# Identity products at TensorE's long waits, wider columns of ones for sums over partitions, and two banks for the keys' tiles

## The chip, the cores and the metric

The kernel runs on one core of one Trainium2 chip. The metric is the device time of one execution in microseconds (us). The time before is 1876.21 us, the median of three runs (1876.06 to 1876.23).

## What is computed

The reference runs 256 tokens of width 1024 through two blocks in float32:

```python
def first_block(x, c, ...):                       # two layers
    for i in range(2):
        mod = silu(c) @ mod_w[i] + mod_b[i]       # shifts, scales and gates, 9 x 1024
        x = x + 0.5 * g1 * swiglu(modulate(rmsnorm(x), sh1, sc1), w13, w2)
        m = pool_ssd_mixer(h, ...) if i == 0 else mla_mixer(h, ...)
        x = x + g2 * m
        x = x + 0.5 * g3 * swiglu(modulate(rmsnorm(x), sh3, sc3), w13, w2)
    return rmsnorm(x, final_norm_g)

def second_block(x, mem, ...):
    x = x + hybrid_mixer(rms_norm(x, norm_mix_g), ...)   # convolution, compressed, selected and window attention
    x = x + cross_attention(rms_norm(x, norm_x_g), mem, ...)
    x = x + swiglu_2(rms_norm(x, norm_ffn_g), ...)
    return rms_norm(x, final_norm_g)
```

So the work is a chain of stages: a normalization, a product with streamed weights, something between the heads or channels, a product back, and the sum into x. Nothing of a stage can begin before x of the stage ahead is whole.

## The kernel before, in words

**Weights.** All weights come as one stream of blocks of 128 x 1024 numbers. SyncE loads them into a ring of six places (`raw`). ScalarE writes the rounded high part `w_hi` (L183, `split_hi`), VectorE the rest `w_lo` (L189, `split_lo`). A product of float32 accuracy is three matmuls in the float32r format (`triple`, L753): high by high, low by high, high by low. ScalarE may split block h only when block h - 6 has been multiplied (semaphore `used`), and SyncE may load over a place only when its low part has been taken. Every engine has one queue, in the order in which the program is written. In the second block, VectorE's queue also holds the 31 taps of a convolution along the tokens (`taps`, L2593 and L2597), three for each block of weights, written between the splits by `next_taps`.

**A normalization** (`norm_x` and `turn`) needs the squares of x (ScalarE), two steps on GpSimd for the root, and a diagonal matrix of the roots for each half of the tokens: the first from ScalarE (L509), the second from VectorE (L521). TensorE multiplies x by that diagonal, 8 tiles for each half (L621), which turns and scales it at once. VectorE and ScalarE take the tiles out of PSUM in pairs and split them (L643 to L682), and the next product starts at the first pair. In three of the normalizations TensorE also sums a block of modulations over the partitions between the two halves (`mod_turn`, L351): the moving operand there is one column of ones. TensorE's first instruction of a normalization waits for the first diagonal; what lies ahead of it in the queue is the last product of the stage before.

**The state-space mixer** of layer 0 handles eight parts n (four quads of heads, two halves of the tokens). For each n, TensorE spreads the running sums (`sums_on_all_rows`, L1571), runs half a block of another product (`z_half`), waits for VectorE's decays (L1614) and multiplies them (`outputs`, L1637 and L1640). After the last one come the sums of squares over the partitions (`group_sums`, L1731) and the roots on all rows (`group_scale`, L1755), in the middle of the product back (`rows_product`).

**The second block's mixer.** `columns_product` multiplies eight convolution pairs, two pairs for the compressed keys and values, then the two sets of keys (`evac_keys`, L2633: four copies on ScalarE for one pair) and the queries. It takes banks ps4 and ps5 in turn by `pair % 2`, counted anew in each call, so two calls of one pair each both take ps4. Then come the products of the compression (`L2664`, 60 columns, and `L2668`, one column), two products for the values, the scores against the compressed keys (L2802, 15 columns), their softmax on VectorE and ScalarE (L2823 to L2854), its transposes (L2866), and 32 passes of attention (`pass_scores`, `pass_turn` L2961, `pass_values` L2980 and L2983), each with half a block of another product (`fill_half`). Within the passes the squares of the convolution are summed by one column of ones (`deviation_sums`, L3044). After the last pass the convolution's channels are split (`conv_split`, L3117) for the next product.

## Time and profile before

| | before |
|---|---|
| median of three runs | 1876.21 us |
| the profiled execution's own time | 1879.29 us |
| its span, first to last instruction | 1877.4 us |
| TensorE busy | 1747.7 us (93%) |
| VectorE busy | 1253.4 us (67%) |
| ScalarE busy | 880.9 us (47%) |
| mean granted TensorE clock | 0.968 |

Busy times are sums over an engine's instructions, and a matmul's end is modelled, so TensorE's 93% is not a share of its peak. [...] A float32 product of a 128 x 128 tile (the L621, L351, L1731 and L3044 kinds) stands in the trace as two records.

### The profile page before, as it was taken

The numbers are of one execution on the slowest core, as the hardware profiler recorded it, in microseconds if no ns is written. First come the engines' busy times: TensorE is split into PE (matmuls) and PEld (weight loads), VectorE is DVE, ScalarE is ACT, GpSimd is POOL, SyncE is SP. The second block draws the span as 40 slices with busy tenths as digits, with TensorE's granted clock in tenths as the row PEclk, the third lists the DMA queues.
The fourth block names the chain that finished last, engine by engine and source line by source line (L and its number), as shares of the span: only waits on it lengthen the run. The fifth ranks groups of instructions, "written<-read, shape, count | busy, mean of one in ns | idle before, by whom it ended". The sixth has DMA issues, their size and how long they took to land.

```text
span 1877.4 us, 32609 instructions
## 1 busy us (share of the span) xinstructions
PE 1747.7 (93%) x11926; PEld 1601.4 (85%) x11926; DVE 1253.4 (67%) x2120; ACT 880.9 (47%) x1412; POOL 72.0 (4%) x119
## 2 busy tenths in 40 slices
PE   4899999799999999999989999898999899899998
PEld 4799988778999889998778999788977688779997
DVE  5777878558778778766556555599785465455554
ACT  1444457534444434444664444545255554554443
POOL 1000001100000000000000000100000000000000
PEclk9999999989999999999999999899799999999999
DMA  9798857647988688854335655344332155326652
GB/s 349 252 304 294 288 140 199 138 163 250 305 296 288 175 324 300 292 170 135 113 91 156 190 183 182 129 146 148 106 92 72 46 180 180 112 79 207 185 184 73
DMA packets 123655, 352.75 MB, mean 188 GB/s; under 512 B 9850, under 2 KB 52874, under 8 KB 114224
## 3 DMA queue, kind: packets, MB, share of 16 engines
q1 hardware_dynamic: 108128, 262.18, 44.3%
q10 hardware_dynamic: 12432, 78.65, 12.3%
q0 software_dynamic: 3008, 10.74, 1.7%
q8 instruction: 58, 0.95, 0.2%
q14 instruction: 29, 0.24, 0.0%
HBM read 347.31 MB, written 4.22 MB: 187 GB/s over the span
## 4 chain that ended last, share of the span: by engine, by line
PE 75%; DVE 13%; ACT 6%; issue 4%; DMA 2%; POOL 1%; ACTq 0%; DVEq 0%; POOLq 0%
PE ps L753 64%; DVE w_lo L189 3%; ACT w_hi L183 2%; DVE arena L2597 2%; PE ps L621 2%; PE ps L2983 1%; PE ps L351 1%; PE ps L2903 1%; DVE arena L342 1%; DMA arena<-in_small 1%; DVE resid L1166 1%; DMA arena<-in_mod_w 1%; PE ps L2961 1%; DVE tmp L1163 0%; DVE act_s L1163 0%
## 5 line engine op out<-in xcount | busy, mean ns | idle before, releaser
L753 PE MATMUL ps<-t_hi,w_hi 128*128 128x256 f32 (+1 forms) x2616 | 757.7, 290 | 21.1 <-DVE arena L2597 5.3
L753 PE MATMUL ps<-t_hi,w_lo 128*128 128x256 f32 (+1 forms) x2616 | 748.9, 286 | 0.0
L753 PE MATMUL ps<-t_lo,w_hi 128*128 128x256 f32 (+1 forms) x2616 | 748.9, 286 | 0.0
L753 PEld LDWEIGHTS ps<-t_hi,w_hi 128*128 128x128 f32 (+1 forms) x2616 | 507.8, 194 | 39.5 <-issue 18.0
L753 PEld LDWEIGHTS ps<-t_lo,w_hi 128*128 128x128 f32 (+1 forms) x2616 | 508.5, 194 | 2.1
L753 PEld LDWEIGHTS ps<-t_hi,w_lo 128*128 128x128 f32 (+1 forms) x2616 | 508.3, 194 | 0.3
L1027 DVE TENSOR_TENSOR w_lo<-raw,w_hi 128x1024 fp32r<-128x1024 f32 x258 | 313.8, 1224 | 155.8 <-ACT w_hi L1016 155.8
L189 DVE TENSOR_TENSOR w_lo<-raw,w_hi 128x1024 fp32r<-128x1024 f32 x240 | 289.7, 1225 | 176.6 <-ACT w_hi L183 176.5
L1016 ACT ACTIVATE w_hi<-raw 128x1024 fp32r<-128x1024 f32 x258 | 269.2, 1053 | 175.1 <-PE ps L753 174.7
L183 ACT ACTIVATE w_hi<-raw 128x1024 fp32r<-128x1024 f32 x240 | 249.0, 1053 | 154.2 <-PE ps L753 129.4
L753 PE MATMUL ps<-w_hi,g_hi 128*128 128x512 f32 x440 | 175.7, 399 | 6.2 <-DVE g_lo L1058 6.1
L342 DVE SCALAR_TENSOR_TENSOR arena<-arena,cact 128x512 f32<-128x512 f32 x231 | 173.2, 750 | 5.1
L753 PE MATMUL ps<-w_hi,g_lo 128*128 128x512 f32 x440 | 172.2, 391 | 0.0
L753 PE MATMUL ps<-w_lo,g_hi 128*128 128x512 f32 x440 | 171.7, 390 | 0.0
L1034 ACT ACTIVATE act_s<-ps 128x256 f32<-128x256 f32 x110 | 42.1, 383 | 194.4 <-PE ps L753 194.4
L753 PE MATMUL ps<-w_hi,t_hi 128*128 128x512 f32 (+1 forms) x272 | 106.1, 390 | 3.4 <-ACT arena L2185 1.5
L753 PEld LDWEIGHTS ps<-w_hi,g_hi 128*128 128x128 f32 x440 | 82.8, 188 | 25.0 <-issue 9.1
L753 PE MATMUL ps<-w_lo,t_hi 128*128 128x512 f32 (+1 forms) x272 | 103.1, 379 | 0.0
L753 PE MATMUL ps<-w_hi,t_lo 128*128 128x512 f32 (+1 forms) x272 | 103.0, 379 | 0.0
L2597 DVE SCALAR_TENSOR_TENSOR arena<-arena,cols 128x256 f32<-128x256 f32 x240 | 99.2, 491 | 0.0
L753 PEld LDWEIGHTS ps<-w_lo,g_hi 128*128 128x128 f32 x440 | 82.7, 188 | 17.9
L1036 ACT ACTIVATE g_hi<-act_s 128x256 fp32r<-128x256 f32 x110 | 45.9, 417 | 110.7 <-DVE act_s L1055 110.7
(337 smaller groups left out, 1656.6 us busy)
## 6 DMA issues: line engine op xcount, KB each, us to landing
raw<-in_stream SPq DMA_DIRECT2D x498, 512.0 KB, 4.4
arena<-in_mod_w ACTq DMA_DIRECT2D x72, 1024.0 KB, 7.2
grow<-gate_scratch POOLq DMA_DIRECT2D x6, 512.0 KB, 9.0
u_scratch<-u_keep ACTq DMA_DIRECT2D x1, 3072.0 KB, 33.8
arena<-u_scratch POOLq DMA_DIRECT2D x8, 256.0 KB, 3.3
small<-in_small POOLq DMA_DIRECT2D x1, 1368.0 KB, 24.9
resid<-in_x POOLq DMA_DIRECT2D x1, 1024.0 KB, 17.0
arena<-in_mem POOLq DMA_DIRECT2D x1, 1024.0 KB, 5.6
```

The source lines that it names most:

```text
L183: E.activation(w_hi[:, s, :], raw[:, s, :], ACT.Copy).then_inc(hi_done, 1)
L189: VE.tensor_tensor(w_lo[:, s, :], raw[:, s, :], w_hi[:, s, :].bitcast(F32), ALU.subtract).then_inc(lo_done, 1)
L342: VE.scalar_tensor_tensor(out=total, in0=w, scalar=cact[:, k:k + 1], in1=total, op0=ALU.mult, op1=ALU.add).then_inc(mod_step, 1)
L351: last = TE.matmul(ps[7][:, at + j:at + j + 1], total[:, j * P:(j + 1) * P], cs("ones", 0, 1), start=True, stop=True)
L621: last = TE.matmul(in_bank(kt)[:, q * P:(q + 1) * P], src(q)[:, kt * P:(kt + 1) * P], rstd_diag[:, q, :], start=True, stop=True)
L753: last = TE.matmul(out, lhs, rhs, start=start and i == 0, stop=stop and i == 2)
L1016: E.activation(w_hi[:, s, :], raw[:, s, :], ACT.Copy).then_inc(hi_done, 1)
L1027: VE.tensor_tensor(w_lo[:, s, :], raw[:, s, :], w_hi[:, s, :].bitcast(F32), ALU.subtract).then_inc(lo_done, 1)
L1034: E.activation(act_s[:, t, 0:L], ps[4 + t][:, 0:L], ACT.Silu).then_inc(silu_done, 1)
L1036: E.activation(g_hi[:, t, :], act_s[:, t, L:2 * L], ACT.Copy).then_inc(gate_hi, 1)
L1166: VE.tensor_tensor(x[:, q, fs], x[:, q, fs], product[:, f, :], ALU.add).then_inc(V.sem, V.up())
L2597: VE.scalar_tensor_tensor(out=cv[:, tile, :], in0=cin[:, tile, k:k + L], scalar=col("dw_w", 8 * k + tile), in1=cv[:, tile, :], op0=ALU.mul ...
```

## The change

It puts four things into TensorE's queue or takes them out:

- `keep_busy(bank, n)` multiplies the identity by itself n times into a bank that nobody reads. It stands ahead of the wait in seven of the normalizations (8, 4, 8, 8, 20, 40 and 36 times), in the state-space parts 1 to 6 (5 each) and 7 (12), at the group sums (6), at the scores (12, and three times 2 between them), at the turns of passes 0 and 31 (6 each) and ahead of the convolution's last product (26). These are 228 products.
- The sums over the partitions use 64 columns of ones (modulations) or 128 (the rest) in place of one. The readers take every 64th or 128th column.
- The compression's one-column products read 60 columns, and 24 of 32 score products 30 columns in place of 15; the added columns are not read.
- The second set of keys takes ps5 (`shift=1`).

```diff
-            total, at = (modp_first[c], 4 * c) if first else (modp, place)
+            total = modp_first[c] if first else modp
             for j in range(4):
-                last = TE.matmul(ps[7][:, at + j:at + j + 1], total[:, j * P:(j + 1) * P], cs("ones", 0, 1), start=True, stop=True)
+                at, wide = (4 * c + j, 1) if first else (place + 64 * j, 64)
+                last = TE.matmul(ps[7][:, at:at + wide], total[:, j * P:(j + 1) * P], cs("ones", 0, wide), start=True, stop=True)
...
                     if kt == 0 and qs[0] == 0:
+                        keep_busy(ps[4], busy)
                         pe.wait_ge(A.sem, entry[1])
...
+        def keep_busy(bank, n):
+
+            for _i in range(n):
+                TE.matmul(bank[:, 0:P], ident, ident, start=True, stop=True)
...
-                bank = ps[4 + pair % 2]
+                which = (pair + shift) % 2
+                bank = ps[4 + which]
...
                 else:
                     pe.wait_ge(A.sem, small_at["state"])
+                if n == 7:
+                    pe.wait_ge(V.sem, less_at[6])
+                if n:
+                    keep_busy(ps[3 if n < 7 else 6], 5 if n < 7 else 12)
                 pe.wait_ge(V.sem, decay_at[n])
...
+                keep_busy(ps[6], 6)
                 pe.wait_ge(A.sem, max(square_at[3], rows_at[7]))
...
-                            last = TE.matmul(ps[7][:, 2 * g + q:2 * g + q + 1], zT[:, 4 * g + i, q * P:(q + 1) * P],
-                                             cs("ones", 0, 1), start=i == 0, stop=i == 3)
+                            last = TE.matmul(ps[7][:, (2 * g + q) * P:(2 * g + q + 1) * P], zT[:, 4 * g + i, q * P:(q + 1) * P],
+                                             cs("ones"), start=i == 0, stop=i == 3)
...
-        columns_product(2, evac_keys(1), chained=True)
+        columns_product(2, evac_keys(1), chained=True, shift=1)
...
-                    last = TE.matmul(cmp_pos[kind][0:64, 0:1], w, sm("pos", kind * 16 + lp, kind * 16 + lp + 1),
+                    last = TE.matmul(cmp_pos[kind][0:64, 0:60], w, sm("pos", kind * 16 + lp - 59, kind * 16 + lp + 1),
...
+            keep_busy(ps[6], 12)
             pe.wait_ge(A.sem, kcmp_at[0])
...
+                    n_col = N_CMP if h // 4 == 3 else 2 * N_CMP
+                    last = TE.matmul(ps[4 + h % 2][:, c:c + n_col], qT[b:b + 64, h // 2, q * P:(q + 1) * P],
+                                     kcmp[b:b + 64, (h // 4) * N_CMP:(h // 4) * N_CMP + n_col], start=True, stop=True)
+                    if h % 8 == 7 and (q, h) != (QT - 1, HEADS - 1):
+                        keep_busy(ps[6], 2)
...
+                pe.wait_ge(A.sem, pt_kept.get(n - 2, pc_at))
+                if n in (0, N_PASS - 1):
+                    keep_busy(ps[4 + n % 2], 6)
                 pe.wait_ge(V.sem, scaled[n])
-                pe.wait_ge(A.sem, pt_kept.get(n - 2, pc_at))
...
-                        last = TE.matmul(sum_bank(1)[:, q:q + 1], square[:, k, q * P:(q + 1) * P], cs("ones", 0, 1),
+                        last = TE.matmul(sum_bank(1)[:, q * P:(q + 1) * P], square[:, k, q * P:(q + 1) * P], cs("ones"),
...
+                    if (pr, half) == (0, 0):
+                        keep_busy(bank, 26)
                     pe.wait_ge(lo_done, h + 1)
```

`token_sums` (L2027) is widened in the same way as L3044. The places of the seven calls in the normalizations, in the order of the program, are those whose L621 starts at 259, 427, 636, 847, 996, 1197 and 1601 us of the trace before.

The order of TensorE's queue at the normalization ahead of the second block's mixer (L621 at 1197 us). Names are output bank <- operands; a row without a wait stands right behind the one ahead. Before:

```order
L753 MATMUL ps<-w_hi,g_hi 128x512
L753 MATMUL ps<-w_hi,g_lo 128x512
L753 MATMUL ps<-w_lo,g_hi 128x512
L598 UNCONDITIONAL_BRANCH
L621 MATMUL ps<-arena,resid 128x128 [waits vector_steps,scalar_steps]
```

With the change (keep_busy is L755, `triple` L761, the product by the diagonal L624):

```order
L761 MATMUL ps<-w_hi,g_hi 128x512
L761 MATMUL ps<-w_hi,g_lo 128x512
L761 MATMUL ps<-w_lo,g_hi 128x512
L600 UNCONDITIONAL_BRANCH
L755 MATMUL ps<-cst 128x128 x40
L624 MATMUL ps<-arena,resid 128x128 [waits vector_steps,scalar_steps]
```

Forty products without a wait of their own now stand between the feed-forward's last matmul and the wait for the diagonal.

The order of TensorE's queue from the compression's last products to the scores (before):

```order
L2705 MATMUL ps<-arena,small 64x60 [waits scalar_steps]
L2708 MATMUL ps<-small,arena 15x64 [waits scalar_steps]
L2708 MATMUL ps<-small,arena 15x64 x3
L2795 UNCONDITIONAL_BRANCH
L2802 MATMUL ps<-arena 128x15 [waits scalar_steps]
L2802 MATMUL ps<-arena 128x15 x31
```

With the change:

```order
L2723 MATMUL ps<-arena,small 64x60 [waits scalar_steps]
L2726 MATMUL ps<-small,arena 15x64 [waits scalar_steps]
L2726 MATMUL ps<-small,arena 15x64 x3
L2813 UNCONDITIONAL_BRANCH
L755 MATMUL ps<-cst 128x128 x12
L2822 MATMUL ps<-arena 128x30 [waits scalar_steps]
L2822 MATMUL ps<-arena 128x30 x7
L755 MATMUL ps<-cst 128x128 x2
L2822 MATMUL ps<-arena 128x30 x4
L2822 MATMUL ps<-arena 128x15 x4
L755 MATMUL ps<-cst 128x128 x2
```

Twelve identity products stand ahead of the wait for the compressed keys, and two more after every eight score products but the last.

## Rows read from the trace of the kernel before

**Rows 1.** The page: its span and the busy time of each engine.

```profile
span 1877.4 us, 32609 instructions
...
PE 1747.7 (93%) x11926; PEld 1601.4 (85%) x11926; DVE 1253.4 (67%) x2120; ACT 880.9 (47%) x1412; POOL 72.0 (4%) x119
```

**Rows 2.** Windows over the stretches at 0.50: columns from, to, length, busy per engine, PEclk, DMA; then their sum.

```profile
376.81:387.06 10.25, 8.93 (x38) 7.49 (x39) 3.10 (x5) 2.01 (x3) 0.00 (x0) 0.50 0.12 42
...
390.47:397.30 6.83, 6.83 (x21) 5.67 (x22) 0.16 (x1) 0.00 (x0) 1.05 (x1) 0.50 0.24 77
...
663.54:666.95 3.41, 3.41 (x19) 3.41 (x18) 2.43 (x3) 1.16 (x2) 0.00 (x0) 0.50 1.02 425
...
1192.60:1202.84 10.24, 5.64 (x26) 5.67 (x27) 4.01 (x8) 4.70 (x13) 3.71 (x6) 0.50 0.01 2
...
1318.89:1335.96 17.07, 17.07 (x133) 17.05 (x132) 11.50 (x26) 2.61 (x6) 2.25 (x3) 0.50 0.39 118
...
1448.60:1455.43 6.83, 6.83 (x26) 5.09 (x26) 3.60 (x14) 1.86 (x6) 1.67 (x1) 0.50 0.26 77
...
1489.56:1492.97 3.41, 3.20 (x11) 2.10 (x11) 0.15 (x1) 0.49 (x1) 0.00 (x0) 0.50 0.00 0
...
sum 121.60, PE 108.60 PEld 102.37 DVE 54.25 ACT 35.62 POOL 15.49; mean PE 5.17 PEld 4.87 DVE 2.58 ACT 1.70 POOL 0.74
```

**Rows 3.** Timeline, TensorE: start, length, line, shape, records; in brackets idle before and releaser.

```profile
427.14 2.02 PE L621 MATMUL ps<-arena,resid 128*128 128x128 f32 x16 [1.50 <-DVE resid L1166]
...
635.79 3.35 PE L621 MATMUL ps<-arena,resid 128*128 128x128 f32 x16 [2.09 <-DVE resid L1166]
...
996.01 6.41 PE L621 MATMUL ps<-arena,resid 128*128 128x128 f32 x32 [3.48 <-DVE resid L1166]
...
1197.20 6.50 PE L621 MATMUL ps<-arena,resid 128*128 128x128 f32 x32 [6.62 <-ACT arena L509]
```

**Rows 4.** Timeline, VectorE, in the normalization whose transposes start at 1197.20.

```profile
1198.74 0.29 DVE L521 TENSOR_SCALAR arena<-cst,st 128x128 f32<-128x128 f32 x1 [2.54 <-POOL st L498]
...
1201.42 0.48 DVE L643 TENSOR_SCALAR tmp<-ps,cols 128x256 f32<-128x256 f32 x1 [2.39 <-PE ps L621]
```

**Rows 5.** Timeline, TensorE, heads of the state-space stage.

```profile
348.01 0.45 PE L1637 MATMUL ps<-arena 128*64 128x128 f32 x4 [2.01 <-DVE arena L1614]
...
355.21 0.66 PE L1637 MATMUL ps<-arena 128*64 128x128 f32 x8 [0.59 <-DVE arena L1614]
...
361.83 0.45 PE L1637 MATMUL ps<-arena 128*64 128x128 f32 x4 [2.02 <-DVE arena L1614]
...
377.35 0.70 PE L1637 MATMUL ps<-arena 128*64 128x128 f32 x4 [2.75 <-DVE arena L1614]
```

**Rows 6.** Timeline, TensorE, sums by one column of ones, and the next work.

```profile
1444.92 3.73 PE L3044 MATMUL ps<-cst,arena 128*128 128x1 f32 x32
...
1448.51 0.82 PE L2961 MATMUL ps<-cst,act_s 128*128 128x128 f32 x3
```

**Rows 7.** Timeline, TensorE, from the keys to the scores.

```profile
1280.55 0.36 PE L753 MATMUL ps<-t_hi,w_hi 128*128 128x256 f32 x1 [2.63 <-DVE arena L2597]
...
1319.54 3.51 PE L2668 MATMUL ps<-small 128*64 128x1 f32 x32
...
1347.03 4.69 PE L2802 MATMUL ps<-arena 64*128 64x15 f32 x64 [1.96 <-ACT arena L2717]
```

**Rows 8.** Windows, then VectorE's timeline, in the same stage.

```profile
1240.00:1330.00 90.00, 79.62 (x641) 78.23 (x640) 90.00 (x185) 37.29 (x49) 0.95 (x1) 0.90 0.46 145
...
1339.98 1.23 DVE L189 TENSOR_TENSOR w_lo<-raw,w_hi 128x1024 fp32r<-128x1024 f32 x1 [9.60 <-ACT w_hi L183]
...
1353.88 0.61 DVE L2823 TENSOR_TENSOR act_s<-ps,biasc 128x120 f32<-128x120 f32 x2
```

**Rows 9.** Timeline, TensorE, after the softmax and after the last pass.

```profile
1360.71 1.09 PE L2866 MATMUL ps<-cst,act_s 128*128 128x128 f32 x8 [0.94 <-DVE act_s L2854]
...
1497.62 0.55 PE L753 MATMUL ps<-t_hi,w_hi 128*128 128x256 f32 x1 [4.36 <-DVE t_lo L3117]
```

More of the change, by code:

```diff
@@ L358, in mod_add @@
                 else bass.ds(c * 4 + COL["mod_b"][0], 4)
-            VE.tensor_tensor(modc[:, sl], ps[7][:, place:place + 4], cols[:, bl], ALU.add).then_inc(mod_added, 1)
+            sums = ps[7][:, place:place + 256].rearrange("p (a b) -> p a b", b=64)[:, :, 0]
+            VE.tensor_tensor(modc[:, sl], sums, cols[:, bl], ALU.add).then_inc(mod_added, 1)
         @block.scalar
@@ L530, in turn @@
         def turn(src, n_kt, segs=None, scale=None, shift=None, kt0=0, dst=None, ready=None, done=False, mods_before=0, early=4,
-                 columns=None, late_mod=None, late_load=False):
+                 columns=None, late_mod=None, late_load=False, busy=0):
             src_ready = ready or {(q, f): V.n for q in range(QT) for f in range(2)}
@@ L911, in columns_product @@
                 evac(pair, bank)
-                bank_free[pair % 2] = (V.n if V.n > at_v else 0, A.n if A.n > at_a else 0)
+                bank_free[which] = (V.n if V.n > at_v else 0, A.n if A.n > at_a else 0)
                 next_split()
@@ L1169, in _, with norm_x @@
                         x_ready[q, f] = V.n
-        def norm_x(gain, mods=None, ready=None, mods_before=0, early=4, late_mod=None, late_load=False):
+        def norm_x(gain, mods=None, ready=None, mods_before=0, early=4, late_mod=None, late_load=False, busy=0):
             if mods is not None:
@@ L1189, in norm_x @@
                      dst=lambda q: ar(XN, QT, D)[:, q, :], ready=ready or dict(x_ready), done=ready is not None,
-                     mods_before=mods_before, early=early, columns=gain_and_scale, late_mod=late_mod, late_load=late_load)
+                     mods_before=mods_before, early=early, columns=gain_and_scale, late_mod=late_mod, late_load=late_load, busy=busy)
             else:
                 turn(lambda q: x[:, q, :], KT, [(0, D)], lambda k: gain(k, 1), None,
-                     dst=lambda q: ar(XN, QT, D)[:, q, :], ready=dict(x_ready), early=early)
+                     dst=lambda q: ar(XN, QT, D)[:, q, :], ready=dict(x_ready), early=early, busy=busy)
         def mod_at(layer, which):
@@ L1203, in build @@
         ffn(0, FG, PRE, (mod_at(0, 2), 0.5))
-        norm_x(lambda k, n: col("norm_g", 8 + k, n), (mod_at(0, 3), mod_at(0, 4)), early=2, late_mod=PRE + FG - 1)
+        norm_x(lambda k, n: col("norm_g", 8 + k, n), (mod_at(0, 3), mod_at(0, 4)), early=2, late_mod=PRE + FG - 1, busy=8)
         xb = ar(0, 12, 259)
@@ L1738, in _ @@
                 dve.wait_ge(T.sem, at)
-                VE.tensor_scalar(wide, ps[7][:, 0:4], 1.0 / 512, EPS, ALU.mult, ALU.add).then_inc(V.sem, V.up())
+                VE.tensor_scalar(wide, ps[7][:, :].rearrange("p (a b) -> p a b", b=P)[:, :, 0], 1.0 / 512, EPS, ALU.mult,
+                                 ALU.add).then_inc(V.sem, V.up())
             at = V.n
@@ L1915, in _ @@
                         out_done[h] = V.n
-        norm_x(lambda k, n: col("norm_g", 32 + k, n), (mod_at(1, 3), mod_at(1, 4)), early=2)
+        norm_x(lambda k, n: col("norm_g", 32 + k, n), (mod_at(1, 3), mod_at(1, 4)), early=2, busy=8)
         squared = ar(0, 4, 512)
@@ L2016, in square_pair, with sums_of @@
             squared_at[i] = A.n
+        def sums_of(bank, at):
+            return bank[:, at * P:(at + 2) * P].rearrange("p (a b) -> p a b", b=P)[:, :, 0]
         def token_sums(pairs, bank, at, read=0):
@@ L2026, in _ @@
                     for i, tile in enumerate(tiles):
-                        last = TE.matmul(bank[:, at + q:at + q + 1], tile, cs("ones", 0, 1), start=i == 0,
+                        last = TE.matmul(bank[:, (at + q) * P:(at + q + 1) * P], tile, cs("ones"), start=i == 0,
                                          stop=i == len(tiles) - 1)
@@ L2466, in build @@
         add_residual((mod_at(1, 5), 1.0))
-        norm_x(lambda k, n: col("norm_g", 40 + k, n), (mod_at(1, 6), mod_at(1, 7)))
+        norm_x(lambda k, n: col("norm_g", 40 + k, n), (mod_at(1, 6), mod_at(1, 7)), busy=20)
         first_gain = ar(0, D)
@@ L2511, in build @@
         norm_rows(first_gain)
-        norm_x(lambda k, n: col("mix", k, n), early=2)
+        norm_x(lambda k, n: col("mix", k, n), early=2, busy=40)
         qT = ar(0, KT, L)
@@ L2675, in _ @@
                 act.wait_ge(T.sem, cmp_mm[kind])
-                E.activation(zk[0:64, 60:61], cmp_pos[kind][0:64, 0:1], ACT.Copy).then_inc(A.sem, A.up())
+                E.activation(zk[0:64, 60:61], cmp_pos[kind][0:64, 59:60], ACT.Copy).then_inc(A.sem, A.up())
                 act.wait_ge(A.sem, A.n)
@@ L2801, in _ @@
                     c = q * 256 + (h // 2) * 32
-                    last = TE.matmul(ps[4 + h % 2][:, c:c + N_CMP], qT[b:b + 64, h // 2, q * P:(q + 1) * P],
-                                     kcmp[b:b + 64, (h // 4) * N_CMP:(h // 4 + 1) * N_CMP], start=True, stop=True)
+                    n_col = N_CMP if h // 4 == 3 else 2 * N_CMP
[3 more added lines that the diff above has]
+                        keep_busy(ps[6], 2)
             last.then_inc(T.sem, T.up())
@@ L3256, in build @@
         evac_rows(vx, ACT.Copy)
-        norm_x(lambda k, n: col("nx", k, n))
+        norm_x(lambda k, n: col("nx", k, n), busy=36)
         columns_product(8, evac_q(qx))
```

18 lines of the change are left out of this document (9 added, 9 removed).

## The prediction

> **What bounds the kernel now.** I read the page first: TensorE is busy 93% of the span, VectorE 67%, ScalarE 47% [rows 1]. So TensorE's queue sets the time, except where it waits. [...] The stretches lie behind waits and behind one-column sums. The timeline then says, stretch by stretch, who is late: the diagonal of a normalization [rows 3], VectorE's decays [rows 5], the taps in VectorE's queue [rows 7, 8]. Two prices follow. At half clock 26 records of L621 fill 5.64 us [rows 2], 0.217 each. The 32 one-column records of L3044 run 1444.92 to 1448.51 at full clock, 0.112 each [rows 6]; 128-column L621 records at full clock I take at the same. So wider ones cost TensorE nothing, and an identity product (two records) costs 0.224 us at full clock, 0.434 at half: 228 of them are 51 us. They are free only inside a wait. That decides each place.
>
> **The change, part by part** (gain positive).
>
> *Normalizations.* At 1197.20 the first copy out of PSUM, which starts the next product, begins at 1201.42, 4.22 after the first L621 [rows 4]. It needs 18 records, and 4.22 less 18 x 0.217 leaves 0.31. At full clock the same is 18 x 0.112 + 0.31 = 2.33. The second diagonal is ready 1.83 after the start (1199.03) [rows 4], so it does not gate. Full clock is worth 1.9. Against it stands the overrun, fills less wait. Eight fills (1.8) fit the wait of 2.09 at 636, where the clock fell just behind the start [rows 2, 3]; two more places, 259 and 847, have the same kind of wait. I take 1.5 each, 4.5 together. Four fills (0.9) fit the 1.50 at 427, where nothing was slow: 0. Twenty (4.5) overrun the 3.48 at 996 by 1.0: +0.9. Forty (9.0) overrun 6.62 by 2.3: -0.4. I take the same -0.4 for the 36 at 1601. Sum **4.6**. Should a fill be shorter than 0.224, the two long ones gain.
>
> *State-space.* Of the two late stretches TensorE fills 8.93 + 6.83 = 15.8 us [rows 2], worth 7.9. Twelve fills (2.7) fit the wait of 2.75 [rows 5]; six at the group sums (1.3) I charge in full. Two of the 21 windows, 3.41 us each, lie in earlier parts, and a part with one took 7.20 (348.01 to 355.21) against 6.62 without (355.21 to 361.83) [rows 5]: 0.6 each. Five fills (1.1) fit the waits near 2.0 and overrun the one of 0.59 by 0.5, which I charge once, as the next wait takes up the rest. 7.9 - 1.3 + 1.2 - 0.6 = **7.2**.
>
> *Columns of ones.* The fall at 663.54 comes right behind the modulations' one-column sums, with 3.41 us of work in it [rows 2]: **1.5**. A like one lies behind the latent's sums (L2027): **1.4**. At 1448.60 the clock falls right behind L3044, with no idle ahead [rows 6]; 6.83 us of busy work follow: **3.1**. VectorE now reads with a stride, 2 to 4 elements: 0.
>
> *Keys to scores.* On TensorE alone much could go: the second set of keys waits 2.63 for its bank [rows 7] and once more alike; two short falls follow, each like the one at 663.54 [rows 2] and worth 1.7; the long stretch from 1318.89 is 17.07 us [rows 2], but of it only the weights' product at the end gains (2.9), since the compression's records are spaced 3.51/32 = 0.110 at half clock [rows 7], the spacing of full clock elsewhere. Together 2 x 2.63 + 2 x 1.7 + 2.9 = 11.6. But VectorE is busy 90.00 of 90 us here [rows 8], with taps and splits in one queue, and what TensorE gains it can only turn into an earlier end of that queue. Its next idle is the 9.60 ahead of 1339.98, released by ScalarE's split, and that by TensorE [rows 8]. When that idle is gone, VectorE's chain from 1339.98 to the softmax at 1353.88, 13.9 us, stays. The ends are 0 (the queue is the bound already) and 9.6 (the idle vanishes). 11.6 exceeds it, so I take **9.6**. The 18 fills there (4.0, wait 1.96) cost nothing while the scores, done at 1351.7 before [rows 7], still end ahead of VectorE's arrival.
>
> *After the softmax.* TensorE, early now, waits longer at L2866 (0.94 before [rows 9]), by what it gains over VectorE: some 4 us, with no fill. I expect the clock to fall there in place of a little later, where it fell before: **0**.
>
> *Passes and end.* The fall at 1489.56 holds 3.20 us of work, the wait of 4.36 ahead of 1497.62 comes behind it [rows 2, 9]. TensorE's and the chain's share of a steady clock is 1.8, the convolution's product itself 0.6 (it is paced by `conv_split`, so 26 fills, 5.8, overrun 4.36 at no price): **2.5**. At pass 0 `pt_kept` and the wait's order change nothing that is late.
>
> Sum 4.6 + 7.2 + 1.5 + 1.4 + 3.1 + 9.6 + 2.5 = 29.9. Every later stage shifts in time, and places without a fill (the latent's short waits, pass 1 onward) may now see a fall: I charge one, 2.0. Gain **27.9**. The profiled execution took 1879.29, span 1877.4; 1851.4 by its count. The median of the runs is 3.1 lower, so **1848.3**. A measurement of this kernel tells some 0.2% (3.8 us) from no change.
>
> [...] The trace's side: from 1192.60 to 1202.84 nothing ran but 26 records of L621, and then the clock rose [rows 2, 3].
>
> **The rivals.**
>
> 1. *VectorE's queue is the bound to the softmax.* For: busy 90.00 of 90 [rows 8]. Against: the idle of 9.60 is there. The keys' term is 0: 1848.3 + 9.6 = 1858. Chance 0.14.
>
> 2. *New falls.* The clock's falls move rather than go, as it does in waits the table of fills leaves out. Four more of 2.2 each (half of 3.4 to 6.8 us [rows 2], less what is hidden): 1857. For: many stretches began behind waits of a microsecond or less. Chance 0.13.
>
> 3. *One-column sums are not what lets the clock fall.* Then the ones give nothing: 1.5 + 1.4 + 3.1 less, 1854.3. [...] Against this rival: [rows 6] has 32 records without a gap and then the fall. Chance 0.08.
>
> 4. *Identity products don't hold the clock (slower).* The mechanism is at the seven normalizations and the other filled waits: the clock falls while they run, so each takes 0.434 and they overrun. Normalizations: 3 x (3.5 - 2.1) + 0.2 for the four at 427 + (8.7 - 3.5) + (17.4 - 6.6) + (15.6 - 5.9) = 30.1; state-space, 12 and 6 fills: 2.4 + 2.6; the last product 11.3 - 4.4 = 6.9. That is 42.0 lost, less 5.3 for the keys' second bank: 1876.2 + 36.7 = 1913. It decides from some 0.39 us per fill on: 162 fills stand where the wait is already full, and 27.9/162 = 0.17 more for each takes the gain. Against it speaks the rise at 1202.84. Chance 0.05.
>
> **How the numbers follow.** The forecast has 0.60. Its own unknowns are the overruns (0 to 4), the shared VectorE chain and the passes' end (0 to 5): 1841 to 1853. Rivals 1 to 3 lie at 1854 to 1858, two of them together at 1863. Nothing prices better than 1838: it needs the whole 11.6 and no overrun and no new fall. So 1838 to 1863 leaves out rival 4 and combinations, some 0.15. Faster by over 0.2% are all but rival 4 and a tail: 0.92; within 0.2% 0.03; slower 0.05.
>
> **What the later profile would show.** Right, if TensorE's mean granted clock rises from 0.968 to 0.99; if the identity products stand 0.112 us per record at clock 1.00; if the diagonal's products in the normalizations start right behind the last fill, with no idle in the long two, and the first copy comes 2.3 after; if L3044 keeps its length with 128 columns and no fall follows; if TensorE has no wait left at the second keys; and if VectorE's idle of 9.60 is gone while the softmax stands 13.9 behind that split. The step after the softmax is right if TensorE waits about 4 us there. The forecast is wrong if the 9.60 stays (rival 1), if stretches at 0.50 sum to more than 40 us (2), if a fall still stands behind the wide sums (3), or if identity products run at 0.217 per record (4).

## The result, and the profile after

| | before | after |
|---|---|---|
| median | 1876.22 us (4 runs, 1876.06 to 1876.71) | 1851.97 us (4 runs, 1850.26 to 1854.25) |
| ratio after to before | | 0.9866, 95% interval 0.9852 to 0.988 |
| the profiled execution's own time | 1879.29 us | 1850.26 us |
| mean granted clock | 0.968 | 0.996 |

The change makes the kernel 24.25 us faster by the medians and 29.0 us faster by the two profiled executions. A second measurement of the changed kernel, beside other kernels on another occasion, gave a median of 1853.85 us.

The page of the changed kernel, its span and busy times, answers to [rows 1]:

```profile
span 1848.4 us, 33513 instructions
PE 1758.8 (95%) x12382; PEld 1615.3 (87%) x12382; DVE 1252.6 (68%) x2120; ACT 880.2 (48%) x1412; POOL 72.6 (4%) x119
```

TensorE has 456 more records (228 identity products) and is busy 11 us longer in a span that is 29 us shorter. In every trace of this case the granted clock is either 1.00 ("full clock" here) or 0.50 ("half clock"). The windows over the stretches at 0.50, which answer to [rows 2]; the columns are those of [rows 2]:

```profile
1200.70:1204.13 3.43, 3.43 (x19) 3.43 (x18) 1.23 (x1) 0.60 (x1) 0.00 (x0) 0.50 0.78 287
1323.60:1333.84 10.24, 10.24 (x62) 9.92 (x63) 10.14 (x23) 0.00 (x0) 0.00 (x0) 0.50 0.47 139
```

Of 121.6 us at half clock, 13.67 are left, and a last stretch from 1845.85 on, behind TensorE's final product (1841.24). The longer one lies at the scores. The window ahead of it:

```profile
1316.78:1323.60 6.82, 6.82 (x76) 6.29 (x76) 6.82 (x15) 5.25 (x10) 0.00 (x0) 1.00 0.36 102
```

TensorE was busy for 6.82 of 6.82 us, mostly with the twelve fills and the first scores of 30 columns, and the clock went from 1.00 to 0.50 at 1323.60 all the same. Without any fills (the first experiment below) a stretch of 10.24 us stands there too, from 1325.17 on. So the fills at the scores show no effect.

TensorE's timeline at the fills and the diagonal's products behind them, in the normalizations that stood at 259, 996, 1197 and 1601 (two of them in [rows 3]):

```profile
258.00 1.95 PE L755 MATMUL ps<-cst 128*128 128x128 f32 x16
260.25 2.02 PE L624 MATMUL ps<-arena,resid 128*128 128x128 f32 x16 [0.30 <-DVE resid L1175]
...
979.16 4.62 PE L755 MATMUL ps<-cst 128*128 128x128 f32 x40
983.63 3.74 PE L624 MATMUL ps<-arena,resid 128*128 128x128 f32 x32
...
1175.80 9.09 PE L755 MATMUL ps<-cst 128*128 128x128 f32 x80
1184.73 3.74 PE L624 MATMUL ps<-arena,resid 128*128 128x128 f32 x32
...
1566.06 8.20 PE L755 MATMUL ps<-cst 128*128 128x128 f32 x72
1574.09 3.74 PE L624 MATMUL ps<-arena,resid 128*128 128x128 f32 x32
```

Eight fills leave 0.30 us of the wait; the long ones leave none. Eighty records take 1184.73 - 1175.80 = 8.93 us, 0.112 each, as priced. The 32 records of the products by the diagonal, 6.50 us before, now take 3.74. ScalarE's first diagonal and VectorE's first copy at 1184.73:

```profile
1182.05 0.40 ACT L511 ACTIVATE arena<-cst,st 128x128 f32<-128x128 f32 x1 [0.37 <-POOL st L500]
```

```profile
1186.94 0.93 DVE L646 TENSOR_SCALAR tmp<-ps,cols 128x256 f32<-128x256 f32 x2 [2.52 <-PE ps L624]
```

The diagonal was ready at 1182.45, the fills ended 2.3 us later, and the first copy comes 2.21 after the first product; the forecast had 2.33. The convolution's sums with 128 columns, TensorE's timeline, answer to [rows 6]:

```profile
1420.88 3.84 PE L3068 MATMUL ps<-cst,arena 128*128 128x128 f32 x32
```

They take 3.84 us in place of 3.73, and no fall follows: the clock is 1.00 from 1333.84 to 1845.85. Last the stage from the keys to the softmax, which answers to [rows 8]: a window, then VectorE's last splits and the softmax.

```profile
1240.00:1330.00 90.00, 86.73 (x763) 85.00 (x763) 90.00 (x185) 41.11 (x59) 3.20 (x4) 0.96 0.48 150
```

```profile
1317.12 1.23 DVE L189 TENSOR_TENSOR w_lo<-raw,w_hi 128x1024 fp32r<-128x1024 f32 x1
...
1331.02 1.18 DVE L2845 TENSOR_TENSOR act_s<-ps,biasc 128x120 f32<-128x120 f32 x4
```

The split that waited 9.60 us has no idle ahead of it, and the softmax starts 13.9 us behind it, as before. VectorE is busy without a break.

**Where the time came from.** VectorE runs the same instructions in the same order in both kernels, so the start of the same instruction, after less before, shows stage by stage what was gained. From the two traces, beside the forecast:

| place | forecast | measured |
|---|---|---|
| normalizations at 259, 636, 847 | 4.5 | 1.5 + 1.4 + 0.8 = 3.7 |
| at 996, 1197, 1601 | 0.9 - 0.4 - 0.4 | 1.3 + 0.1 + 0.7 |
| state-space | 7.2 | 7.2 |
| modulations' and latent's sums | 1.5 + 1.4 | 1.2 + 1.6 |
| a new fall behind L883 (1200.7) | in the 2.0 charged | -1.2 |
| keys to softmax | 9.6 | 9.7 |
| after the softmax | 0 | 0.9 |
| passes, convolution's sums | 3.1 | 3.3 |
| end of the passes | 2.5 | 1.4 |
| sum | 27.9 | 29.0 (0.7 was lost in the first 62 us, 0.1 behind the last place) |

### The profile page after: what moved, and what is told of

It is laid out like the page before. It is cut to its first block, busy times and chain, and to the rows that moved or that the text cites. A ratio compares the mean times of both kernels' runs of the same rounds, so it can differ in the third digit from the quotient of the medians.

```text
span 1848.4 us, 33513 instructions
## 1 busy us (share of the span) xinstructions
PE 1758.8 (95%) x12382; PEld 1615.3 (87%) x12382; DVE 1252.6 (68%) x2120; ACT 880.2 (48%) x1412; POOL 72.6 (4%) x119
## 4 chain that ended last, share of the span: by engine, by line
PE 73%; DVE 14%; ACT 6%; issue 5%; DMA 2%; POOL 0%; ACTq 0%; DVEq 0%; POOLq 0%
PE ps L761 63%; DVE w_lo L189 4%; DVE arena L2615 3%; ACT w_hi L183 2%; PE ps L352 1%; PE ps L755 1%; PE ps L3007 1%; PE ps L2925 1%; DVE arena L342 1%; DMA arena<-in_small 1%; PE ps L624 1%; DMA arena<-in_mod_w 1%; DVE resid L1175 1%; PE ps L2985 1%; ACT t_hi L674 0%
## 5 line engine op out<-in xcount | busy, mean ns | idle before, releaser
L761 PE MATMUL ps<-t_hi,w_hi 128*128 128x256 f32 (+1 forms) x2616 | 751.0, 287 | 14.5 <-DVE t_lo L685 6.1
L761 PE MATMUL ps<-t_lo,w_hi 128*128 128x256 f32 (+1 forms) x2616 | 743.0, 284 | 0.0
L761 PE MATMUL ps<-t_hi,w_lo 128*128 128x256 f32 (+1 forms) x2616 | 742.8, 284 | 0.0
L761 PEld LDWEIGHTS ps<-t_hi,w_hi 128*128 128x128 f32 (+1 forms) x2616 | 502.3, 192 | 31.3 <-issue 14.4
L761 PEld LDWEIGHTS ps<-t_lo,w_hi 128*128 128x128 f32 (+1 forms) x2616 | 502.5, 192 | 2.1
L761 PEld LDWEIGHTS ps<-t_hi,w_lo 128*128 128x128 f32 (+1 forms) x2616 | 502.4, 192 | 0.2
L761 PE MATMUL ps<-w_hi,g_hi 128*128 128x512 f32 x440 | 175.7, 399 | 6.0 <-DVE g_lo L1067 5.7
L761 PE MATMUL ps<-w_hi,g_lo 128*128 128x512 f32 x440 | 172.1, 391 | 0.0
L761 PE MATMUL ps<-w_lo,g_hi 128*128 128x512 f32 x440 | 171.7, 390 | 0.0
L761 PE MATMUL ps<-w_hi,t_hi 128*128 128x512 f32 (+1 forms) x272 | 102.8, 378 | 3.4 <-ACT arena L2203 1.6
L761 PEld LDWEIGHTS ps<-w_hi,g_hi 128*128 128x128 f32 x440 | 82.8, 188 | 25.1 <-issue 9.1
L761 PE MATMUL ps<-w_lo,t_hi 128*128 128x512 f32 (+1 forms) x272 | 100.1, 368 | 0.0
L761 PE MATMUL ps<-w_hi,t_lo 128*128 128x512 f32 (+1 forms) x272 | 100.0, 368 | 0.0
L761 PEld LDWEIGHTS ps<-w_lo,g_hi 128*128 128x128 f32 x440 | 82.6, 188 | 18.1
```

The lines of the kernel that those rows point to most:

```text
L761: last = TE.matmul(out, lhs, rhs, start=start and i == 0, stop=stop and i == 2)
```

## The experiments

Twelve kernels ran, in three groups of four, each group beside runs of the kernel before. That kernel's median was 1878.88, 1875.98 and 1878.97 in the three, with single runs from 1872.99 to 1884.13, so kernels of different groups are compared by their ratio to it. The changed kernel's ratio was 0.9866 first and 0.988 in the second group.

### Take the fills away

```diff
         def keep_busy(bank, n):
-            for _i in range(n):
-                TE.matmul(bank[:, 0:P], ident, ident, start=True, stop=True)
+            return
```

> The changed kernel without its 228 identity products; wide columns and the keys' second bank stay. My theory (the fills hold the clock through their waits): the terms of the normalizations (4.6), most of the state-space stage (4 to 7) and the end of the passes (2.5) are lost: 1863 to 1866, and the profile shows falls to 0.50 again at 259, 636, 847, 996, 1197, 1497 and 1601 of the kernel before. Rival (the fills bring nothing, the wide columns and the bank do it all): 1850 to 1854, with the overruns of the long fills gone.

Measured: 1860.82 us, ratio 0.9911 (0.9883 to 0.9939). The changed kernel's ratios were 0.9866 and 0.988, so the fills are worth 0.3 to 0.45% of the time, 6 to 8 us, less than the 11 to 14 expected. TensorE's timeline in the normalization that stood at 1197, and VectorE's first copy:

```profile
1188.25 5.63 PE L624 MATMUL ps<-arena,resid 128*128 128x128 f32 x32 [6.63 <-ACT arena L511]
```

```profile
1192.35 0.93 DVE L646 TENSOR_SCALAR tmp<-ps,cols 128x256 f32<-128x256 f32 x2 [2.27 <-PE ps L624]
```

The clock falls there again (0.50 from 1185.22 to 1192.05), and the first copy comes 4.10 after the first product in place of 2.21. But the product starts 0.15 behind the diagonal in place of 2.28, since nothing overruns. The forty fills give nothing and cost nothing, close to the term -0.4. Laid over the changed kernel, 8.2 us are lost without the fills: 1.6 at the normalization at 259, 1.6 in the state-space stage, 2.4 between 640 and 685, where the modulations of the next stage are summed, 1.3 at the end of the passes, and the rest in pieces below 1. Of the 2.4, 1.3 stands at a fall (673.23, 3.4 us at 0.50) that the changed kernel's second trace has too (671.03), with its fills. From that first copy to the softmax the time is 144.01 us against 144.08: in that stage the fills do nothing.

At three places where the forecast put the gain down to the fills, it is there without them. TensorE's timeline of this kernel at the normalization that stood at 636 and at the late part of the state-space stage, beside 635.79 in [rows 3] and 377.35 in [rows 5]:

```profile
630.50 2.02 PE L624 MATMUL ps<-arena,resid 128*128 128x128 f32 x16 [2.12 <-DVE resid L1174]
...
377.45 0.45 PE L1649 MATMUL ps<-arena 128*64 128x128 f32 x4 [2.74 <-DVE arena L1622]
```

The waits are as long as before, nothing fills them, and the clock stays at 1.00 (3.35 and 0.70 us before). Against the kernel before, this one gains 1.5 us at 636, 0.8 at 847 and 5.6 in the state-space stage, where the changed kernel gained 1.4, 0.8 and 7.2. My expectation of falls at 636 and 847 missed. Part of the 5.6 is the group sums' 128 columns (1.6, shown below); the rest is not tied to any edit.

### Fills that stream one column

```diff
-                TE.matmul(bank[:, 0:P], ident, ident, start=True, stop=True)
+                TE.matmul(bank[:, 0:1], ident, ident[:, 0:1], start=True, stop=True)
```

> The changed kernel with identity products that stream one column in place of 128; as many records, in the same places. They should stand 0.11 us apart as before. My theory (what counts for the clock is what is streamed, not that the queue is occupied): the clock falls at the filled places as without fills, and the overruns of the long fills stay on top: 1865 to 1870. Rival (occupied time holds the clock): 1850 to 1854.

Measured: 1876.95 us, ratio 0.9986 (0.9972 to 1.0001): hardly faster than before. TensorE's timeline and two windows at the forty fills:

```profile
1186.43 15.06 PE L755 MATMUL ps<-cst 128*128 128x1 f32 x80
1201.36 4.87 PE L624 MATMUL ps<-arena,resid 128*128 128x128 f32 x23
```

```profile
1184.00:1188.62 4.62, 4.62 (x33) 4.19 (x31) 4.51 (x8) 2.17 (x6) 1.21 (x2) 1.00 0.00 0
1188.62:1205.69 17.07, 17.07 (x81) 17.07 (x82) 3.15 (x7) 3.79 (x11) 3.70 (x6) 0.50 0.00 1
```

TensorE is busy without a gap, the clock falls among the fills, at 1188.62, and is 0.50 for 17.07 us. The last 4.3 of them, from 1201.36 on, hold 128-column products. Of the 14.93 us from the first fill to the diagonal's product, 21 records at full clock take 2.4; the other 59 stand 0.213 apart. So the forty end 6 us later than the wide ones. TensorE's queue was occupied here for all of the 17.07 us at 0.50; with the same number of records of 128 columns, at the same place, the clock was 1.00 over the whole 8.93 us. The direction was expected, not the size (1865 to 1870): the forecast for this run took 0.11 us per record at either clock.

### Fills issued as transposes

```diff
-                TE.matmul(bank[:, 0:P], ident, ident, start=True, stop=True)
+                TE.transpose(bank[:, 0:P], ident, ident)
```

> The changed kernel with its fills issued as transposes of the identity in place of plain matmuls by it, the same number and places. [...] If they count as a matmul does: 1850 to 1855 and a clock of 0.99.

Measured: 1849.99 us, ratio 0.9841 (0.9824 to 0.9857). TensorE's timeline, then two windows:

```profile
1180.62 4.53 PE L755 MATMUL ps<-cst 128*128 128x128 f32 x40
1187.41 5.44 PE L624 MATMUL ps<-arena,resid 128*128 128x128 f32 x32 [2.25 <-ACT arena L511]
```

```profile
1184.90:1188.31 3.41, 1.16 (x11) 0.94 (x10) 1.42 (x2) 1.84 (x7) 2.00 (x4) 1.00 0.00 0
1188.31:1191.73 3.42, 3.42 (x19) 3.42 (x18) 0.84 (x3) 0.47 (x1) 0.56 (x1) 0.50 0.02 5
```

A transpose is one record of 0.112 us where the float32 product is two, so forty take half the time and leave an idle of 2.25. The clock is 1.00 for as long as they run and falls only behind that idle. Idle at this place let the clock fall 2.0 us after its start in the kernel before (1190.58 to 1192.60) and 3.6 us after it without fills (1181.62 to 1185.22); here the clock stood for the 7.7 us from 1180.62 to 1188.31, with nothing in them but the transposes, the idle and 0.9 us of L624. So over these 4.53 us the transposes held the clock at 1.00, as the identity products did over their 8.93 in the changed kernel, and the runs (median 1849.99, clocks 0.989 to 0.994) are close to the 1850 to 1855 and 0.99 expected for transposes that count as a matmul does. The kernel is no slower than with the long fills, though the clock falls behind the short ones (0.50 from 1188.31 to 1191.73), which fits the forty being too many.

### One column of ones again

```diff
-                at, wide = (4 * c + j, 1) if first else (place + 64 * j, 64)
+                at, wide = (4 * c + j, 1) if first else (place + 64 * j, 1)
...
-                        last = TE.matmul(sum_bank(1)[:, q * P:(q + 1) * P], square[:, k, q * P:(q + 1) * P], cs("ones"),
+                        last = TE.matmul(sum_bank(1)[:, q * P:q * P + 1], square[:, k, q * P:(q + 1) * P], cs("ones", 0, 1),
```

> The changed kernel with one column of ones again in the four kinds of sums over partitions; the fills, the 60 and 30 columns and the keys' second bank stay. My theory (work that streams one column lets the clock fall, though TensorE has no idle): 1.5 + 1.4 + 3.1 are lost, 1857 to 1859, with falls behind the modulations' sums near 650, the latent's near 856 and the convolution's sums near 1423. Rival (only idle lowers the clock, the wide columns are idle talk): 1850 to 1854 and no fall at those three places.

Measured: 1861.0 us, ratio 0.9902 (0.9877 to 0.9927), 4 to 7 us above the changed kernel (0.988 and 0.9866). TensorE's timeline at the convolution's sums, and the windows around:

```profile
1429.79 3.86 PE L3068 MATMUL ps<-cst,arena 128*128 128x1 f32 x32
1433.51 0.88 PE L2985 MATMUL ps<-cst,act_s 128*128 128x128 f32 x3
```

```profile
1426.00:1433.25 7.25, 7.25 (x56) 6.18 (x55) 2.16 (x12) 3.90 (x11) 0.00 (x0) 1.00 0.29 86
1433.25:1440.08 6.83, 6.83 (x26) 5.09 (x26) 3.55 (x14) 1.87 (x6) 1.67 (x1) 0.50 0.26 77
```

TensorE is busy 7.25 of 7.25 us and the clock falls at 1433.25; with the same 32 records of 128 columns (3.84 us, from 1420.88 on in the changed kernel) it stayed at 1.00. That stage alone lost 3.0 us, the term 3.1. All three traces with one column here have this fall (at 1448.60, 1433.25 and 1444.79, 6.83 us each), and none of the eleven with 128 columns has one. The falls at the group sums (388.77, 1.6 us lost) and the latent's sums (859.81, 1.2 lost), 3.41 us at 0.50 each, came back too.

The one near 650 did not, and for the modulations' sums the runs do not show that the column count is the cause. All traces have a wait of 1.1 us ahead of that sum. With one column the clock fell in one trace of three, with 64 in none of eleven. At the next sum, 17 us on, it fell in eight of the eleven with 64 columns, at waits of 1.45 to 2.77 us, and stood in the three others, at 0.76, 1.13 and 2.19.

The profiled execution is 12.1 us above the changed kernel's. Its other losses stand where this edit changes nothing: 1.3 near 81 us (0.50 from 78.16 to 81.57) and 4.5 from the scores to the first passes, where the clock is 0.50 for 13.65 us.

### The keys in one bank, and narrow compression, singly and together

```diff
-        columns_product(2, evac_keys(1), chained=True, shift=1)
+        columns_product(2, evac_keys(1), chained=True)
```

> The changed kernel with both sets of keys in the same bank again. My theory: VectorE's queue sets the time from the keys to the softmax; without the second bank TensorE loses 2 x 2.63 there, of which VectorE's idle takes a part: 1854 to 1858, and an idle of 2 to 5 us stands again ahead of a low split in VectorE's queue between 1300 and 1320. Rival (the fills and wider columns alone fill VectorE's queue): 1850 to 1854. Rival (the bank is the whole 9.6): 1861.

```diff
-                    last = TE.matmul(cmp_pos[kind][0:64, 0:60], w, sm("pos", kind * 16 + lp - 59, kind * 16 + lp + 1),
+                    last = TE.matmul(cmp_pos[kind][0:64, 59:60], w, sm("pos", kind * 16 + lp, kind * 16 + lp + 1),
...
-                    n_col = N_CMP if h // 4 == 3 else 2 * N_CMP
+                    n_col = N_CMP
```

> The changed kernel with one column again in the compression's second products and 15 in all the scores. No second bank explains more than a part of the 9.6, as the kernel without it showed 2.5. My theory now: most of the rest came from the clock held through the compression; here it falls there again, TensorE's next products are late by 3 to 6 and VectorE's idle ahead of the last splits is back: 3 to 6 above the changed kernel. Rival (VectorE's queue hides it all): 0 to 1 above, with a fall but no idle on VectorE.

Both diffs at once:

> The changed kernel with the keys in one bank and the compression and scores narrow again, both at once. From the first copy of the normalization at 1197 to the softmax it was 152.5 us before, 144.1 with the change, 146.6 without the bank and 145.8 with the narrow columns. Theory (both make slack on TensorE ahead of a VectorE queue that is the bound, and each makes most of it): together more than the sum 2.5 + 1.7, that stretch at 149 to 153 and VectorE's idle back at 6 to 10. Rival (they add): 148.3.

| kernel | median us | ratio (95% interval) | first copy to softmax |
|---|---|---|---|
| before | | 1 | 152.46 |
| changed (second measurement) | 1853.85 | 0.988 (0.9866 to 0.9894) | 144.08 |
| one bank | 1856.03 | 0.9879 (0.9854 to 0.9905) | 146.59 |
| narrow | 1851.77 | 0.9876 (0.9858 to 0.9893) | 145.75 |
| both | 1857.75 | 0.9888 (0.987 to 0.9905) | 148.72 |

The times of whole kernels do not tell these apart, the stage does. VectorE's timeline with one bank, the split ahead of which the idle stands and the softmax:

```profile
1321.38 1.23 DVE L189 TENSOR_TENSOR w_lo<-raw,w_hi 128x1024 fp32r<-128x1024 f32 x1 [2.31 <-ACT w_hi L183]
...
1335.40 0.91 DVE L2845 TENSOR_TENSOR act_s<-ps,biasc 128x120 f32<-128x120 f32 x3
```

The bank is worth 2.5 us, nearly all of it as an idle of VectorE that is back. The narrow columns cost 1.7 there (3 to 6 were expected), though all 17.07 us at half clock are back (1300.07 to 1317.14); VectorE's queue hides most of them. Together they cost 4.6, about the sum, where I had expected more than the sum. So 3.7 of the 8.4 us of this stage come back neither with both edits nor without the fills alone (144.01); all three edits at once weren't tried. The traces say where most of it lies. TensorE's timeline at the compression's second products, before [rows 7], with the change, and with both edits undone:

```profile
1319.54 3.51 PE L2668 MATMUL ps<-small 128*64 128x1 f32 x32
...
1297.63 2.04 PE L2686 MATMUL ps<-small 128*64 128x60 f32 x32
...
1304.55 1.99 PE L2686 MATMUL ps<-small 128*64 128x1 f32 x32
```

Before, both sets of 32 ran at half clock, 3.51 us each. With both edits undone they took 1.99 and 2.15 us, one column or not: 1.5 and 1.4 less. The clock fell mostly between them, from 1306.73 to 1310.14, 0.4 us into the second set, and again at the scores, from 1330.62 on. So where the falls happen to lie decides, and not these two edits alone.

### The changed kernel again, with shorter fills, with fewer taps

```diff
-        norm_x(lambda k, n: col("norm_g", 40 + k, n), (mod_at(1, 6), mod_at(1, 7)), busy=20)
+        norm_x(lambda k, n: col("norm_g", 40 + k, n), (mod_at(1, 6), mod_at(1, 7)), busy=16)
...
-        norm_x(lambda k, n: col("mix", k, n), early=2, busy=40)
+        norm_x(lambda k, n: col("mix", k, n), early=2, busy=30)
...
-        norm_x(lambda k, n: col("nx", k, n), busy=36)
+        norm_x(lambda k, n: col("nx", k, n), busy=27)
```

> The changed kernel, unchanged, as the measure for the other three of this group. Every theory: 1850 to 1855, some 23 to 25 below the kernel before. Its runs should scatter by about 4 us, since the places where the clock falls depend on what happens to lie together.

> The changed kernel with 30, 27 and 16 identity products in place of 40, 36 and 20 in the three longest normalization waits. In the trace of the changed kernel the last fill ends 2.2, 2.0 and 0.9 us after the first diagonal there. My theory (the long fills overrun, and what the clock gives they take): the first copy out of PSUM comes 2.1, 1.9 and 0.9 earlier, 4.9 in all: 4 to 5 below the changed kernel, if the clock does not fall in the rest of the wait. Rival (another engine is as late, or the shorter row lets the clock fall): no gain.

Measured: the changed kernel 1853.85 us (1853.42 to 1854.56), with shorter fills 1850.02 (1848.06 to 1850.7), ratios 0.988 and 0.9856 (0.9842 to 0.9871): 3.8 us less. TensorE's timeline with thirty fills:

```profile
1179.66 6.86 PE L755 MATMUL ps<-cst 128*128 128x128 f32 x60
1186.42 3.94 PE L624 MATMUL ps<-arena,resid 128*128 128x128 f32 x32
```

The clock is 1.00 from the first fill to the end of the products, and the product starts as the fills end. The overrun was real: beside the repeated changed kernel the first copy comes 2.0 us earlier here, and 1.8 us earlier at 1601. The rest of the difference is not the fills' alone. This trace has a fall in the state-space stage that the other lacks (0.50 from 351.76 to 355.17, 2.1 us lost), and it lacks the one behind L883 (0.50 from 1203.51 to 1206.93 in the other, 1.5 gained), though the wait there is the same 1.80 us:

```profile
1201.64 0.32 PE L883 MATMUL ps<-cst,tmp 48*128 48x48 f32 x2 [1.80 <-ACT act_s L2584]
```

After the softmax, though, TensorE's timeline of this run and of the repeated changed kernel shows what I forecast there and what the first profile did not have (a wait of 1.20 and no fall):

```profile
1338.25 1.97 PE L2888 MATMUL ps<-cst,act_s 128*128 128x128 f32 x8 [4.56 <-DVE act_s L2876]
```

```profile
1339.80 1.56 PE L2888 MATMUL ps<-cst,act_s 128*128 128x128 f32 x7 [2.72 <-DVE act_s L2876]
```

Behind both waits the clock is 0.50 for 6.8 us. Another fall that the first profile lacks stands in the repeated run behind a wait of 1.45 us at the modulations' wide sums; TensorE's timeline, then the window behind it:

```profile
669.37 1.10 PE L352 MATMUL ps<-cst,arena 128*128 128x64 f32 x8 [1.45 <-DVE arena L342]
```

```profile
671.03:674.45 3.42, 3.42 (x10) 2.68 (x9) 2.43 (x3) 0.96 (x2) 0.00 (x0) 0.50 1.02 405
```

The third kernel of this comparison takes taps out of VectorE's queue:

```diff
         def three_taps():
-            for _i in range(3):
+            tap_calls[0] += 1
+            for _i in range(2 if tap_calls[0] % 4 == 0 else 3):
                 next_taps()
```

> The changed kernel with two taps instead of three after every fourth block of weights; the taps left out there are written later, in the passes. My theory (VectorE's queue sets the time from the convolution pairs to the softmax): some 8 to 10 taps of 0.8 us leave it, and the time falls until TensorE is the bound: 2 to 5 us less than the changed kernel. Rival (the queue is not the bound, or the passes pay it back): within 1 us of the changed kernel.

Measured: 1846.51 us (1845.37 to 1848.38), ratio 0.9843 (0.9831 to 0.9856): 7.3 us less than the changed kernel, more than expected. VectorE's softmax and TensorE's product behind it:

```profile
1326.96 1.16 DVE L2848 TENSOR_TENSOR act_s<-ps,biasc 128x120 f32<-128x120 f32 x4
```

```profile
1334.12 1.04 PE L2891 MATMUL ps<-cst,act_s 128*128 128x128 f32 x8
```

First copy to softmax takes 137.0 us in place of 144.1, and TensorE no longer waits behind the softmax. VectorE's busy time in this stage fell by the same 7.1 us (135.6 to 128.5, 18 instructions fewer), and its idle stayed at 11.1. The queue of VectorE was the bound of this stage, and the passes had room for the taps.

### The same taps in the kernel before

> The kernel before with only the taps spread (two after every fourth block). Theory: there TensorE's bank waits and its half clock are the later ones, VectorE idles 9.6 ahead of 1340, and fewer taps in front gain at most the bank waits' part that comes from the queue (the wait of 2.63 ends with a tap): 0 to 5 of the 7.1 that they gained behind the change. Rival (VectorE's queue was the bound before as well): 6 to 8 below the kernel before.

Measured: 1870.84 us, 8 us less by the medians; by the ratio, 0.9963 (0.9948 to 0.9977), 7 us less (4 to 10). VectorE's timeline:

```profile
1336.34 1.23 DVE L189 TENSOR_TENSOR w_lo<-raw,w_hi 128x1024 fp32r<-128x1024 f32 x1 [8.11 <-ACT w_hi L183]
...
1349.46 1.14 DVE L2826 TENSOR_TENSOR act_s<-ps,biasc 128x120 f32<-128x120 f32 x4
```

First copy to softmax is 145.0 against 152.5, a gain of 7.5, though the idle of 8.11 stays; my expectation of 0 to 5 missed. But the taps did not bring all of it themselves. TensorE's products stand 2.3 us earlier by 1258.93, where its waits for taps shrink (from 1.34 to 0.54 us each). Some 4 us more come between 1294.8 and 1331.7, where 17.07 us at half clock are 6.83 in this trace. TensorE's timeline there, beside 1319.54 in [rows 7]:

```profile
1320.09 2.03 PE L2671 MATMUL ps<-small 128*64 128x1 f32 x32
```

So behind the change the queue was a bound of 7.1 us; in the kernel before it held TensorE up by 2.3, and whether the fall moved because of the taps or by chance no run shows. That the two stage gains add up to 7.5 + 8.4 is therefore no proof of two separate bounds.

### The three that helped, together

The diffs of the shorter fills and of the taps, and:

```diff
         def narrow_turn(n, bank):
             @block.tensor
             def _(pe):
+                keep_busy(ps[6], 8)
                 pe.wait_ge(A.sem, A.n)
```

> The changed kernel with the shorter fills (30, 27, 16), the spread taps, and eight identity products ahead of the wait of 1.8 us in front of the gates' transposes (L883). The two former gave 3.8 and 7.3 on their own, at places that don't touch; the fill takes away the fall behind L883, whose 3.4 us at half clock are worth up to 1.7, but VectorE or TensorE may hide it. If they add: 1853.9 - 11.1 = 1842.7, less 0 to 1.5: 1841 to 1843. If they share one bound: 1845 to 1847.

Measured: 1842.52 us (1839.6 to 1846.51), ratio 0.9806 (0.9789 to 0.9824), 36 us below the kernel before and clearly below the changed one (0.9866 and 0.988). TensorE's timeline at the added fills:

```profile
1196.17 1.95 PE L755 MATMUL ps<-cst 128*128 128x128 f32 x16
1198.13 0.32 PE L884 MATMUL ps<-cst,tmp 48*128 48x48 f32 x2
```

The wait of 1.8 us is filled, no fall stands behind it (the clock is 1.00 up to 1320.54), and first copy to softmax is 135.5, 1.5 less than with the taps alone. That the fill did this is not shown: with the shorter fills alone the fall was missing too, behind an unfilled wait. The gains of shorter fills and taps add, within the intervals (0.9856 and 0.9843 against 0.988 make 0.982 together). In its profiled execution one stretch of 3.4 us at half clock is left, at the scores (1320.54), beside the one behind TensorE's final product (from 1832.54).

## Why the prediction was right, and where it was off

- **The forecast held, in part by luck**: 1848.3 was forecast, 1851.97 measured, inside 1838 to 1863. By the profiled executions 27.9 us were forecast and 29.0 came. The fills, though, are worth 6 to 8 us where the terms that rest on them (4.6, 7.2 and 2.5) add up to 14.3. The total came out because most of those places gained even without fills.
- **The 3.7 us between forecast and median** come from one step: "The median of the runs is 3.1 lower, so 1848.3". I carried the kernel before's distance of profile and median over to the changed kernel. The changed kernel's profiled execution was the fastest of its four, 1.7 below its median. 3.1 + 1.7 = 4.8 is the difference between 29.0 and 24.25, and the profiled gain was 1.1 above the forecast.
- **Normalizations**: right in price (0.112 per record, first copy 2.21 after the start against 2.33) and in kind (the long fills overrun). The term for the forty, -0.4, came out near 0 (0.1 in the table); the fills begin 0.2 before the last matmul's modelled end, so the overrun costs less. The shorter fills confirmed the overrun, with 2.0 and 1.8 us at the two longest. At 259 the fills are the cause (1.6). At 636 and 847 the gain came without them. Where the prediction takes some half of a stretch's work as the gain of full clock, the records show about that: 0.217 us apart at half clock [rows 2], 0.112 at full.
- **State-space**: 7.2 forecast and measured, but the fills are worth 1.6 of it and the wide group sums 1.6, which the prediction did not name. That the clock falls at the late wait unless it is filled was wrong: in the kernel without fills it stayed at 1.00 behind 2.74 us. What the remaining 4 us hang on stays open.
- **Columns of ones**: the convolution's term (3.1) has its cause shown, 3.0 lost with one column at the same place. The latent's 1.4 came back as 1.2. For the modulations' 1.5 the cause is not shown.
- **Keys to scores**: 9.6 forecast, 9.7 measured: the idle vanished and 13.9 us of chain stayed. The pieces were off. The second bank is worth 2.5, not 2 x 2.63. And the prediction took 0.110 us for the compression's records as the spacing of full clock too, so it put their half clock at nothing; at full clock 32 of them take 2.0 us in place of 3.51. What I had not seen is that, once the idle is gone, VectorE's queue is a bound worth 7 us more. Rival 1 had that fact right (90.00 of 90) and drew the wrong sum from it.
- **After the softmax**: the wait of some 4 us with a fall came in two later profiles (2.72 and 4.56), not in the first.
- **End of the passes**: 2.5 forecast, 1.4 measured. The fills there give 1.3 of it, as the kernel without them showed; what the rest hangs on is not shown.
- **New falls** (rival 2) did come, one in the first profile (behind L883, at 1200.70) and three in the repeated one (there, at 1203.51, at 671.03, and after the softmax, at 1340.05). Its "many stretches" behind waits of a microsecond or less were fewer: in the kernel before three of the 21 have a wait of that size in the 5 us ahead of them, 0.61, 0.75 and 1.07 us (at 1489.56, 1318.89 and 663.54). My charge of 2.0 was about right for the first and too little for the second. **Rival 3** fell with the one-column sums for the convolution; its sign, a fall behind wide sums, did come at the modulations' (671.03). **Rival 4** fell with the price of a fill (0.112 us per record, where it had 0.217) and the clock of 1.00 over the forty.

## What to carry to other kernels

Read the stretches at half clock first and ask of each what TensorE streamed ahead of it. Here the clock fell in waits (in the one of 6.62 us at 1197, 2.0 us after its start) and behind one-column products (the 32 records of 3.73 us at 1444.92), and at full clock 128 columns cost hardly more time than one (3.84 against 3.73 us for 32 records). Fill a wait with products of all columns (forty of 128 columns ran at 1.00 for 8.93 us here; with one column the clock fell 2.2 us after the first), but no longer than the wait: what ran over it cost 2.0 and 1.8 us at the two longest. Then take the fills away again: a fall that has gone may have gone for another reason, and a total that agrees with the forecast does not show which term brought it. Where an engine's queue is busy without a break, lighten the queue as well and measure the stage by itself.

## What the runs showed of the hardware that was not expected

- One-column float32 records stand 0.112 us apart at full clock and 0.213 at half, as in the fills of one column (1186.43 to 1201.36). The compression's products, whose stationary tile has 64 columns in place of 128, stood 0.110 apart at half clock [rows 7] and 0.063 at full (32 in 2.03 us).
- With the same work the clock falls at different places from run to run: the changed kernel's second trace has falls at 671.03 (3.42 us) and 1340.05 (6.82 us) that the first lacks, and the kernel before had medians of 1876 to 1879 and single runs from 1873 to 1884. A difference of 2 us between kernels is told by a stage of the trace, not by their medians.
- Forty transposes of 128 x 128 float32 numbers stood as 40 records in 4.53 us (0.112 us apart), forty products by the identity as 80 in 8.93 us.
